# First weights ahead of the activations, their parts on two DMA queues, and the row norm spread inside the third tile

## The chip, the core and the metric

The kernel runs on one core of a Trainium2 chip. The metric is the device time of one execution in microseconds (us); of three runs the median counts. A core has five engines that run their own instruction streams and meet at semaphores: TensorE (PE, matrix products), VectorE (DVE), ScalarE (ACT), GpSimd (POOL) and SyncE (SP), which here only issues DMAs. "PEld" is the load of the stationary matrix of a product.

## The reference

Two small blocks of layers run one after the other on a sequence of 256 tokens (272 with 16 meta tokens in the first), with a model width of 1024, all in float32. What matters here is how the first block begins:

```python
h = jnp.concatenate([meta, x], axis=1)               # 272 x 1024
u = rmsnorm(h, mix_norm[layer])                      # x * rsqrt(mean(x^2) + eps) * gain
z = jnp.einsum('bld,de->ble', u, w_in[e])
hq, hf, hi, hg, cq, ckv, kr = jnp.split(z, IN_SPLITS, axis=-1)
o_a = hgrn2_mixer(hq, hf, hi, hg, lower_bounds[e], hgrn_out_norm[e])
o_b = mla_mixer(cq, ckv, kr, ...)
mix = jnp.einsum('ble,ed->bld', jnp.concatenate([o_a, o_b], axis=-1), w_out[e])
```

`hgrn2_mixer` turns `hf` into a decay (absolute values, exponentials, logarithms), sums it along the sequence in one scan, and works on chunks of 64 positions in levels of 1, 2, 4, 8, 16 and 32. Everything after this stage (the MLPs, a pooling layer, and the second block with a convolution and an attention) is some 1100 us of matrix products with the same helpers.

## The kernel before

**Layout.** The activations stand transposed: `X` is 128 x 8 x 272, the feature in the partition and in the middle index `j`, the token along the row. A product in float32 is made of three in a faster format: `UH` holds the high part of x times gain, `UL` the rest, and each weight unit is split into `WH` and `WL`. `products` (L367) issues for each of 8 blocks `k` the three matmuls UH,WH, UL,WH and UH,WL, so 24 matmuls of 272 columns to a 128-column tile of the result.

**Weights.** Weights come in units of up to 128 x 1024 floats (512 KB), one for each tile. Unit n goes by DMA from `wpack` into one of 4 buffers `RAW` (`load_unit`, L336), ACT copies it into one of 7 buffers `WH` (`act_split`, L345), and DVE writes `WL` = RAW - WH (`dve_split`, L352). The load of unit n waits until `WL` of unit n-4 is written. All of SP's DMAs are issued in the order of its program.

**The root.** The division by the root mean square comes after the product. ACT squares x in four pieces (`square`, L435), DVE adds them up (`add_squares`, L445), and PE sums over the partitions with matmuls against a column of ones (`root_begin` and `root_end`, through L449). ACT takes the square root (L480, L481), DVE the reciprocal (L487, L488), PE spreads it over all partitions (`root_spread`, L495), ACT copies it into `RR` (`root_keep`, L503). A tile's result is then multiplied by `RR` on its way out of PSUM (`divided`, L1061). Its 8 banks of PSUM are handed out in turn.

**The order at the start.** SP issues x whole, the gains, an identity matrix, then units 0 to 3 and a table of constants `C`. ACT waits for x, then works through squares, the eight `UH`, the root, `RR`, and only then splits units 0 to 3. DVE follows in the same order. PE makes the sums, the spread, and then the tiles: hf 0 to 3, hq 0 to 3, cq 0 and 1, ckv 0, the first attention level, ckv 1, and so on, with one level after every further tile. Behind the hf tiles a chain on ACT and DVE forms the decay (L936 to L951, L1257 to L1275), then the scan (L1278), then six rounds of exponents and operands for the levels (L1070 to L1109).

`keep_going(t, n)` (L398) issues n matmuls of ones by ones, 256 columns wide, whose result nobody reads. `preload` (L507) is a one-column activation that makes ACT load its table early. `act_split(a, n)` and `dve_split(v, n)` split all units below n that are not yet split.

Of the kernel before, what the change touches and what calls it, by code (L numbers as in the profile page):

```python
# [8 lines left out]
T = 272  # L9
# [3 lines left out]
NR = 4  # L13
# [92 lines left out]
NG = _at  # L106
# [171 lines left out]
def program(nc, xin, pin, gains, cst, wpack, out):  # L278
# [13 lines left out]
    with ctx:  # L292
# [28 lines left out]
        def g(name, j=0, p=128):  # L321
            return G[0:p, GAT[name] + j:GAT[name] + j + 1]
# [8 lines left out]
        def load_unit(s, n):  # L331
            w = width(units[n])
            src = wpack[offs[n]:offs[n] + 128 * w].rearrange("(p n) -> p n", p=128)
            if n >= NR:
                s.wait_ge("wl", n - NR)
            s.e.dma_start(RAW[n % NR][:, 0:w], src).then_inc(*s.mark_dma(f"raw{n % NR}", n))  # L336
# [135 lines left out]
        def root_sum(t, st, i, w, freed):  # L472
            root_begin(t, st, i, w, freed)
            root_end(t, st, i, w)
# [43 lines left out]
        def sync_start(s):  # L518
            s.e.dma_start(X[:, :, :], xin).then_inc(*s.mark_dma("x"))
            s.e.dma_start(G[:, :], gains).then_inc(*s.mark_dma("g"))  # L520
            s.e.dma_start(ID[:, :], cst[:, CAT["id"]:CAT["id"] + 128]).then_inc(*s.mark_dma("id"))
            for n in range(NR):
                load_unit(s, n)

# [77 lines left out]
        def tensor_mixer(t):  # L602
            u_ready = (lambda k: ("ul", "m", k))

            def project(key, js, freed):
                for j in js:
                    n = unit_at[key, j]
                    z = len(units[n][4])
                    b = banks.take(t, (key, j), (freed, key, j))
                    products(t, PS[0:z, b, 0:T], n, pairs, 0, z, xh_full, xl_full, u_ready).then_inc(*t.mark("mix", key, j))  # L610
                    sig.also(("used", n), ("mix", key, j))

            def values(uu, i):
# [166 lines left out]

            root_sum(t, "m", 0, T, ("rk", "m"))
            root_spread(t, "m", T)
            project("hf", range(4), "ev")
            project("hq", range(4), "ev")
# [94 lines left out]
        def scalar_mixer(a):  # L879
# [41 lines left out]

            a.wait_ge("g")
            a.wait_ge("ones", 2)
            a.wait_ge("x")
            for p in range(4):
                square(a, "m", 0, p, X[:, 2 * p:2 * p + 2, :], T)
            for j in range(8):
                split_hi(a, ("m", j), UH[:, j, :], X[:, j, :], g("mix0", j))
            root_sqrt(a, "m", T)
            root_keep(a, "m", 0, T)  # L930
            act_split(a, 4)
            a.wait_ge("lb", 0)
# [124 lines left out]
        def vector_mixer(v):  # L1057
# [169 lines left out]

            v.wait_ge("g")
            v.wait_ge("x")
            for p in range(4):  # L1230
                add_squares(v, "m", 0, p, T)
            for j in range(8):
                split_lo(v, ("m", j), UL[:, j, :], X[:, j, :], g("mix0", j), UH[:, j, :])
            root_recip(v, "m", T)
            lbg = G[:, GAT["lb"]:GAT["lb"] + 4]
            v.e.tensor_tensor(LO, lbg, lbg, ALU.subtract).then_inc(*v.mark("lb", 0))
            dve_split(v, 4)
            v.wait_ge("rr", "m")
# [1472 lines left out]
        def sync_program(s):  # L2711
            sync_start(s)
            s.e.dma_start(C[:, :], cst[:, 128:NCA]).then_inc(*s.mark_dma("c"))
            for n in range(NR, NU):
                load_unit(s, n)
            for p in range(4):
                s.wait_ge("x2", "end", p)
                s.e.dma_start(out[:, 2 * p:2 * p + 2, :], X[:, 2 * p:2 * p + 2, NM:T]).then_inc(*s.mark_dma("out", p))
            s.wait_ge("out", 3)
# [95 lines left out]
```

## Time and profile before

| | us |
|---|---|
| three runs | 1288.32, 1290.06, 1290.20 |
| median | 1290.06 |
| the profiled execution, its own time | 1293.58 |
| its span, first to last instruction | 1291.7 |
| PE busy | 1255.8 |
| DVE busy | 896.4 |
| ACT busy | 739.2 |

Busy time of an engine says how full it is over the whole program; which engine is waited for changes from stage to stage. Times in the rows further down are counted from the first instruction. In a timeline a row with xN is N instructions of one kind in a row, its second number is their time together, and consecutive instructions overlap a little, so the step from one start to the next is shorter than one instruction's duration. What stands in brackets is the idle time before the row and what ended it.

### The profile page before, as it was taken

To read this page: it belongs to the slowest core of one execution; us is meant where nothing else is said; L and a number is where in the kernel's file an instruction comes from. 1 tells how busy PE (TensorE), PEld (TensorE's weight loads), DVE (VectorE), ACT (ScalarE), POOL (GpSimd) and SP (SyncE) were. 2 spreads that over 40 slices of the span, in tenths; PEclk is the share of its full clock that TensorE was granted. 3 is DMA by queue.
4 is the path that set the end of the run, shared out by engine and by line. 5 is a ranking of instruction groups with operands and counts; after the bars stand their busy time and mean duration, and the time that the engine had idled before them with its cause. 6 is when DMAs were issued, how large, how long until landed. Compare 5 with 4: busy or idle time off the path is not lost.

```text
span 1291.7 us, 24686 instructions
## 1 busy us (share of the span) xinstructions
PE 1255.8 (97%) x10317; PEld 1232.7 (95%) x10317; DVE 896.4 (69%) x1549; ACT 739.2 (57%) x1262; POOL 6.4 (0%) x16
## 2 busy tenths in 40 slices
PE   5999999999999999999999999999999999999997
PEld 5989889999999999999999999999999899999997
DVE  4896456765456666444775799965788767999655
ACT  5854355654445666334545666664766766665644
POOL 1000000000000000000000000000000000000000
PEclk9999799999999999999999999999999999999999
DMA  6223124655553565554564566665364335655630
GB/s 246 94 82 115 65 82 147 213 169 190 166 164 114 193 184 184 190 181 154 180 197 131 171 196 194 190 205 163 101 207 164 103 115 169 197 192 186 217 118 34
DMA packets 58891, 205.54 MB, mean 159 GB/s; under 512 B 6515, under 2 KB 8860, under 8 KB 58524
## 3 DMA queue, kind: packets, MB, share of 16 engines
q1 hardware_dynamic: 57104, 201.77, 47.9%
q10 hardware_dynamic: 1676, 2.19, 0.6%
q8 instruction: 82, 1.34, 0.4%
q14 instruction: 29, 0.24, 0.1%
HBM read 202.87 MB, written 1.06 MB: 158 GB/s over the span
## 4 chain that ended last, share of the span: by engine, by line
PE 87%; ACT 5%; DVE 5%; DMA 1%; issue 1%; ACTq 0%; DVEq 0%
PE PS L367 70%; PE PS L415 6%; PE PS L378 2%; PE PS L449 2%; DVE WL L352 1%; ACT WH L345 1%; PE PS L398 1%; PE PS L2301 1%; PE PS L495 1%; ACT EE L2459 1%; ACT L507 1%; PE PS L637 1%; PE PS L2368 0%; PE PS L668 0%; DMA RAW<-wpack 0%
## 5 line engine op out<-in xcount | busy, mean ns | idle before, releaser
L352 DVE TENSOR_TENSOR WL<-RAW,WH 128x1024 fp32r<-128x1024 f32 (+2 forms) x385 | 460.4, 1201 | 218.8 <-ACT WH L345 218.4
L345 ACT ACTIVATE WH<-RAW 128x1024 fp32r<-128x1024 f32 (+2 forms) x385 | 392.4, 1038 | 230.6 <-PE PS L367 197.3
L367 PE MATMUL PS<-UH,WH 128*128 128x256 f32 (+2 forms) x1576 | 447.4, 284 | 3.5 <-DVE WL L352 2.7
L367 PE MATMUL PS<-UH,WL 128*128 128x256 f32 (+2 forms) x1576 | 447.2, 284 | 0.0
L367 PE MATMUL PS<-UL,WH 128*128 128x256 f32 (+2 forms) x1576 | 447.2, 284 | 0.0
L367 PEld LDWEIGHTS PS<-UH,WH 128*128 128x128 f32 (+1 forms) x1576 | 297.8, 189 | 4.3 <-DVE WL L352 3.0
L367 PEld LDWEIGHTS PS<-UH,WL 128*128 128x128 f32 (+1 forms) x1576 | 298.1, 189 | 0.0
L367 PEld LDWEIGHTS PS<-UL,WH 128*128 128x128 f32 (+1 forms) x1576 | 296.3, 188 | 0.0
L367 PE MATMUL PS<-HL,WH 128*128 128x272 f32 (+1 forms) x512 | 145.8, 285 | 0.0
L367 PE MATMUL PS<-HH,WH 128*128 128x272 f32 (+1 forms) x512 | 145.7, 285 | 0.0
L367 PE MATMUL PS<-HH,WL 128*128 128x272 f32 (+1 forms) x512 | 145.4, 284 | 0.0
L367 PE MATMUL PS<-FH,WH 128*128 128x256 f32 x352 | 98.6, 280 | 0.0
L367 PE MATMUL PS<-FL,WH 128*128 128x256 f32 x352 | 98.5, 280 | 0.0
L367 PE MATMUL PS<-FH,WL 128*128 128x256 f32 x352 | 98.4, 280 | 0.0
L367 PEld LDWEIGHTS PS<-HH,WL 128*128 128x128 f32 x512 | 96.6, 189 | 0.0
L367 PEld LDWEIGHTS PS<-HL,WH 128*128 128x128 f32 x512 | 96.3, 188 | 0.0
L367 PEld LDWEIGHTS PS<-HH,WH 128*128 128x128 f32 x512 | 96.1, 188 | 0.0
L415 PE MATMUL PS<-UH,WH 128*128 128x256 f32 (+1 forms) x256 | 74.1, 290 | 1.2 <-DVE UL L515 1.0
L415 PE MATMUL PS<-UH,WL 128*128 128x256 f32 (+1 forms) x256 | 72.0, 281 | 0.0
L415 PE MATMUL PS<-UL,WH 128*128 128x256 f32 (+1 forms) x256 | 72.0, 281 | 0.0
L367 PEld LDWEIGHTS PS<-FH,WH 128*128 128x128 f32 x352 | 66.2, 188 | 0.0
L367 PEld LDWEIGHTS PS<-FL,WH 128*128 128x128 f32 x352 | 66.2, 188 | 0.0
(392 smaller groups left out, 1931.8 us busy)
## 6 DMA issues: line engine op xcount, KB each, us to landing
RAW<-wpack SPq DMA_DIRECT2D x363, 512.0 KB, 3.8
RAW<-wpack SPq DMA_DIRECT2D x16, 384.0 KB, 3.5
RAW<-wpack SPq DMA_DIRECT2D x6, 256.0 KB, 2.6
X<-xin SPq DMA_DIRECT2D x1, 1088.0 KB, 5.0
C<-cst SPq DMA_DIRECT2D x1, 1072.0 KB, 10.0
HB<-bias_rows ACTq DMA_DIRECT2D x1, 1024.0 KB, 6.2
out<-X SPq DMA_DIRECT2D x4, 256.0 KB, 2.3
VF<-cst ACTq DMA_DIRECT2D x1, 512.0 KB, 3.8
```

The costliest lines, as they stand in the source:

```text
L345: a.e.activation(WH[n % NH][:, 0:w], RAW[n % NR][:, 0:w], ACT.Copy).then_inc(*a.mark("wh", n))
L352: v.e.tensor_tensor(WL[n % NH][:, 0:w], RAW[n % NR][:, 0:w], WH[n % NH][:, 0:w].bitcast(f32), ALU.subtract).then_inc(*v.mark("wl", n))
L367: ins = t.e.matmul(o, part(n, hw, kw, a, b), x(kx), start=first and not i and not p, stop=last and i == len(kcs) - 1 and p == 2)
L378: ins = t.e.matmul(o, x(kx), part(n, hw, kw, 0, w), start=not i and not p, stop=i == len(kcs) - 1 and p == 2)
L398: t.e.matmul(PS[:, b, 0:256], ONER[:, :], ONER[:, :].unsqueeze(1).to_broadcast([128, 2, 128]), start=True, stop=True)
L415: ins = t.e.matmul(PS[:, b, 0:w], part(n, hw, k, 0, 128), x_(k), start=k == 0 and p == 0, stop=k == 7 and p == 2)
L449: return t.e.matmul(o, src[:, m, a:z], ONE[:, 0:1], start=first and m == 0, stop=last and m == 1)
L495: ins = t.e.matmul(PS[:, b, a:z], rooted(st, x).to_broadcast([128, 128]), ID[:, 0:z - a], start=True, stop=True)
L507: a.e.activation(SM[:, 60:61], EPS[:, 0:1], func)
L637: ins = t.e.matmul(PS[:, b + x // 4, 128 * (x % 4):128 * (x % 4) + 128], kb[:, hh, a:z], qb[:, hh, a:z], start=True, stop=True)
L2301: ins = t.e.matmul(PS[:, b, 0:256], x[:, k, 128 * i:128 * i + 128], part(n, hw, kw, 0, 256), start=k == 0 and p == 0, stop=k == 7 and p == 2)
L2459: ins = a.e.activation(e, e, ACT.Exp, bias=s[:, 2 * i + m:2 * i + m + 1], scale=-1.0, accum_out=s[:, 4 + 2 * i + m:5 + 2 * i + m])
```

## The change

The change touches only the beginning.

- SP issues unit 0, then the second quarter of x, unit 1, the fourth quarter, the identity matrix, unit 2, the rest of the gains, unit 3. The table `C` moves behind unit 5.
- ACT issues three DMAs of its own: the eight columns of the gains that the first norm needs, and the first and third quarter of x. It then loads the table of the square root, splits unit 0, and makes the eight `UH`, with unit 1 split after the sixth. Squares come after that, then units 2 and 3, then the root.
- DVE takes the same order: unit 0, the eight `UL`, unit 1, the sums of squares, units 2 and 3, the reciprocal.
- PE begins with 24 matmuls of ones, makes tile hf 0 with one matmul of ones between two blocks and six behind it, then hf 1, the sums of the root (with 4 matmuls of ones in their midst), hf 2 with the spread in its middle, hf 3, and goes on as before.

```diff
         def sync_start(s):
-            s.e.dma_start(X[:, :, :], xin).then_inc(*s.mark_dma("x"))
-            s.e.dma_start(G[:, :], gains).then_inc(*s.mark_dma("g"))
+            load_unit(s, 0)
+            s.e.dma_start(X[:, 2:4, :], xin[:, 2:4, :]).then_inc(*s.mark_dma("xp1"))
+            load_unit(s, 1)
+            s.e.dma_start(X[:, 6:8, :], xin[:, 6:8, :]).then_inc(*s.mark_dma("xp3"))
             s.e.dma_start(ID[:, :], cst[:, CAT["id"]:CAT["id"] + 128]).then_inc(*s.mark_dma("id"))
-            for n in range(NR):
-                load_unit(s, n)
+            load_unit(s, 2)
+            s.e.dma_start(G[:, 8:NG], gains[:, 8:NG]).then_inc(*s.mark_dma("g"))
+            load_unit(s, 3)
...
+            def first_tile():
+                b = banks.take(t, ("hf", 0), ("ev", "hf", 0))
+                for k in range(8):
+                    ins = products(t, PS[:, b, 0:T], unit_at["hf", 0], [(k, k)], 0, 128, xh_full, xl_full, u_ready, k == 0,
+                                   k == 7)
+                    if k < 7:
+                        keep_going(t, 1, done=("ones",))
...
+                keep_going(t, 6, done=("ones",))
+            def tile_with_root():
...
+                products(t, PS[:, b, 0:T], n, pairs[0:4], 0, 128, xh_full, xl_full, u_ready, True, False)
+                root_spread(t, "m", T)
+                products(t, PS[:, b, 0:T], n, pairs[4:8], 0, 128, xh_full, xl_full, u_ready, False, True).then_inc(
...
-            root_sum(t, "m", 0, T, ("rk", "m"))
-            root_spread(t, "m", T)
-            project("hf", range(4), "ev")
+            t.wait_ge("ones", 0)
+            keep_going(t, 24)
+            first_tile()
+            project("hf", (1,), "ev")
+            root_begin(t, "m", 0, T, ("rk", "m"))
+            keep_going(t, 4, done=("ones",))
+            root_end(t, "m", 0, T)
+            tile_with_root()
+            project("hf", (3,), "ev")
...
-            a.wait_ge("g")
-            a.wait_ge("ones", 2)
-            a.wait_ge("x")
+            a.e.dma_start(G[:, 0:8], gains[:, 0:8]).then_inc(*a.mark_dma("gm"))
+            for p in (0, 2):
+                a.e.dma_start(X[:, 2 * p:2 * p + 2, :], xin[:, 2 * p:2 * p + 2, :]).then_inc(*a.mark_dma(f"xp{p}"))
+            preload(a, ACT.Sqrt)
+            act_split(a, 1)
+            a.wait_ge("gm")
+            for j in range(8):
+                a.wait_ge(f"xp{j // 2}")
+                split_hi(a, ("m", j), UH[:, j, :], X[:, j, :], g("mix0", j))
+                if j == 5:
+                    act_split(a, 2)
             for p in range(4):
                 square(a, "m", 0, p, X[:, 2 * p:2 * p + 2, :], T)
-            for j in range(8):
-                split_hi(a, ("m", j), UH[:, j, :], X[:, j, :], g("mix0", j))
+            act_split(a, 4)
+            a.wait_ge("ones", 2)
             root_sqrt(a, "m", T)
             root_keep(a, "m", 0, T)
-            act_split(a, 4)
+            a.wait_ge("g")
...
+            dve_split(v, 1)
+            v.wait_ge("gm")
+            for j in range(8):
+                v.wait_ge(f"xp{j // 2}")
+                split_lo(v, ("m", j), UL[:, j, :], X[:, j, :], g("mix0", j), UH[:, j, :])
+            dve_split(v, 2)
             for p in range(4):
                 add_squares(v, "m", 0, p, T)
-            for j in range(8):
-                split_lo(v, ("m", j), UL[:, j, :], X[:, j, :], g("mix0", j), UH[:, j, :])
+            dve_split(v, 4)
             root_recip(v, "m", T)
+            v.wait_ge("g")
...
             for n in range(NR, NU):
                 load_unit(s, n)
+                if n == NR + 1:
+                    s.e.dma_start(C[:, :], cst[:, 128:NCA]).then_inc(*s.mark_dma("c"))
```

The instructions of ACT, from its first on, in the program before. `WH<-RAW` is the split of a weight unit, `UH<-X,G` the high part of x times gain, `ACC` and `SQ` are the squares, `RS` the root; in brackets is what the row waits for:

```order
L435 ACT_TABLE_LOAD [waits s_x,s_ones]
L435 ACTIVATE ACC<-X 128x544 [waits s_g]
L435 ACTIVATE SQ<-X 128x544 x2
L435 ACTIVATE SQ<-X 128x544 [waits s_acc]
L511 ACTIVATE UH<-X,G 128x272 x8
L480 ACT_TABLE_LOAD
L480 ACTIVATE RS<-PS,EPS 16x1 [waits s_sum]
L481 ACTIVATE RS<-PS,EPS 128x2
L503 ACTIVATE RR<-PS 128x272 [waits s_rsp]
L345 ACTIVATE WH<-RAW 128x1024 [waits s_raw0]
```

And ACT in the changed program, from its first split on (its three DMA issues and the load of the table stand before it):

```order
L345 ACTIVATE WH<-RAW 128x1024 [waits s_raw0]
L511 ACTIVATE UH<-X,G 128x272 [waits s_xp0,s_gm]
...
L511 ACTIVATE UH<-X,G 128x272
L345 ACTIVATE WH<-RAW 128x1024 [waits s_raw1]
L511 ACTIVATE UH<-X,G 128x272 [waits s_xp3]
L511 ACTIVATE UH<-X,G 128x272
L435 ACTIVATE ACC<-X 128x544
L435 ACTIVATE SQ<-X 128x544 x2
L435 ACTIVATE SQ<-X 128x544 [waits s_acc]
L345 ACTIVATE WH<-RAW 128x1024 [waits s_raw2]
L345 ACTIVATE WH<-RAW 128x1024 [waits s_raw3]
L480 ACTIVATE RS<-PS,EPS 16x1 [waits s_sum,s_ones]
```

Units 0 to 3 moved ahead of the root, the squares behind the `UH`, and one of the two table loads is gone.

PE from its first matmul on, in the program before (`ONE,ACC` and `ONE,SQ` are the sums of the root, `ID,RS` is its spread, `UH,WH` the first matmul of tile hf 0):

```order
L449 MATMUL PS<-ONE,ACC 128x1 [waits s_acc]
L449 MATMUL PS<-ONE,ACC 128x1 x3
L449 MATMUL PS<-ONE,SQ 128x1 [waits s_sq]
L449 MATMUL PS<-ONE,SQ 128x1 x3
L449 MATMUL PS<-ONE,ACC 16x1 x2
L449 MATMUL PS<-ONE,SQ 16x1 x2
L495 MATMUL PS<-ID,RS 128x16 [waits s_id,s_rr]
L495 MATMUL PS<-ID,RS 128x128 x2
L367 MATMUL PS<-UH,WH 128x272 [waits s_ul,s_wl]
```

PE in the changed program at the same sums, which now stand between tiles hf 1 and hf 2 (`ONE` are the matmuls of ones, the last row the first matmul of hf 2):

```order
L449 MATMUL PS<-ONE,ACC 128x1 [waits s_acc]
L449 MATMUL PS<-ONE,ACC 128x1 x3
L398 MATMUL PS<-ONE 128x256 x4
L449 MATMUL PS<-ONE,SQ 128x1 [waits s_sq]
L449 MATMUL PS<-ONE,SQ 128x1 x3
L449 MATMUL PS<-ONE,ACC 16x1 x2
L449 MATMUL PS<-ONE,SQ 16x1 x2
L367 MATMUL PS<-UH,WH 128x272 [waits s_wl]
```

Before, these sums and the spread stood ahead of the first tile; now two tiles, or 48 matmuls, run before them.

## Rows read from the trace of the kernel before

**Rows 1.** The page, part 1: busy time by engine.

```profile
PE 1255.8 (97%) x10317; PEld 1232.7 (95%) x10317; DVE 896.4 (69%) x1549; ACT 739.2 (57%) x1262; POOL 6.4 (0%) x16
```

**Rows 2.** Waits of PE, 0 to 170 us: us in total, times, longest.

```profile
PE PS L449 <- DVE ACC L445: 10.1, 1, 10.1
PE PS L367 <- DVE WL L352: 2.7, 1, 2.7
```

**Rows 3.** The chain that ended last, from the start: start us, us, what.

```profile
0.74 5.03 DMA X<-xin
...
13.22 1.28 ACT L480
...
19.55 34.80 PE PS L367 x264
...
73.91 0.72 DVE KB L1085
...
93.14 2.84 PE PS L668 x24
```

**Rows 4.** Windows at the start: PE busy, PEclk, DMA share, GB/s.

```profile
3.00:4.00 1.00, 0.00 (x0) 1.00 1.00 418
...
20.00:21.00 1.00, 1.00 (x6) 1.00 0.40 90
```

**Rows 5.** The page, part 6: DMA issues, KB each, us to landing.

```profile
RAW<-wpack SPq DMA_DIRECT2D x363, 512.0 KB, 3.8
```

**Rows 6.** Timeline, 9 to 23 us: start us, us, engine line op.

```profile
9.81 3.39 ACT L511 ACTIVATE UH<-X,G 128x272 fp32r<-128x272 f32 x8
...
15.21 1.65 PE L495 MATMUL PS<-ID,RS 128*128 128x16 f32 x6 [1.24 <-DVE RS L488]
...
17.19 3.88 ACT L345 ACTIVATE WH<-RAW 128x1024 fp32r<-128x1024 f32 x4
18.27 4.63 DVE L352 TENSOR_TENSOR WL<-RAW,WH 128x1024 fp32r<-128x1024 f32 x4 [3.05 <-ACT WH L345]
...
19.95 0.43 PE L367 MATMUL PS<-UL,WH 128*128 128x272 f32 x1
...
20.17 0.43 PE L367 MATMUL PS<-UH,WL 128*128 128x272 f32 x1
...
22.54 0.29 PE L367 MATMUL PS<-UL,WH 128*128 128x272 f32 x1
...
22.66 0.29 PE L367 MATMUL PS<-UH,WL 128*128 128x272 f32 x1
```

**Rows 7.** Timeline of DVE, 33 to 50 us.

```profile
33.20 0.44 DVE L1061 TENSOR_TENSOR LF<-PS,RR 128x272 f32<-128x272 f32 x1 [1.45 <-PE PS L367]
...
39.25 0.44 DVE L1061 TENSOR_TENSOR Q<-PS,RR 128x272 f32<-128x272 f32 x1 [2.58 <-PE PS L367]
...
48.33 1.29 DVE L1275 TENSOR_TENSOR LF<-LF,B 128x1088 f32<-128x1088 f32 x1 [0.20 <-ACT B L951]
```

**Rows 8.** Timeline of ACT, 33 to 45 us.

```profile
33.68 1.11 ACT L936 ACTIVATE B<-LF 128x1088 f32<-128x1088 f32 x1 [1.07 <-DVE LF L1061]
...
44.11 1.11 ACT L948 ACTIVATE B<-B 128x1088 f32<-128x1088 f32 x1 [0.17 <-DVE B L1266]
```

**Rows 9.** Waits of DVE, 39 to 94 us: us in total, times, longest.

```profile
DVE KB L1085 <- PE PS L643: 0.9, 2, 0.6
```

**Rows 10.** Timeline of PE, near the program's end.

```profile
1278.26 1.36 PE L398 MATMUL PS<-ONE 128*128 128x256 f32 x10
...
1279.46 0.95 PE L449 MATMUL PS<-ONE,ACC 128*128 128x1 f32 x8
```

**Rows 11.** Windows of 2 us: PE busy, PEclk, DMA share, GB/s.

```profile
136.00:138.00 2.00, 2.00 (x17) 1.00 0.65 205
...
140.00:142.00 2.00, 2.00 (x10) 0.50 0.56 221
...
152.00:154.00 2.00, 2.00 (x9) 0.98 0.00 0
```

More of the change, by code:

```diff
@@ L611, in project @@
                     sig.also(("used", n), ("mix", key, j))
+            def first_tile():
[5 more added lines that the diff above has]
+                        keep_going(t, 1, done=("ones",))
+                ins.then_inc(*t.mark("mix", "hf", 0))
+                sig.also(("used", unit_at["hf", 0]), ("mix", "hf", 0))
+                keep_going(t, 6, done=("ones",))
+            def tile_with_root():
+                n = unit_at["hf", 2]
+                b = banks.take(t, ("hf", 2), ("ev", "hf", 2))
+                products(t, PS[:, b, 0:T], n, pairs[0:4], 0, 128, xh_full, xl_full, u_ready, True, False)
+                root_spread(t, "m", T)
+                products(t, PS[:, b, 0:T], n, pairs[4:8], 0, 128, xh_full, xl_full, u_ready, False, True).then_inc(
+                    *t.mark("mix", "hf", 2))
+                sig.also(("used", n), ("mix", "hf", 2))
             def values(uu, i):
@@ L1226, in normed @@
                     *v.mark("rope", "k"))
-            v.wait_ge("g")
-            v.wait_ge("x")
+            dve_split(v, 1)
[4 more added lines that the diff above has]
+            dve_split(v, 2)
             for p in range(4):
                 add_squares(v, "m", 0, p, T)
-            for j in range(8):
-                split_lo(v, ("m", j), UL[:, j, :], X[:, j, :], g("mix0", j), UH[:, j, :])
+            dve_split(v, 4)
             root_recip(v, "m", T)
+            v.wait_ge("g")
             lbg = G[:, GAT["lb"]:GAT["lb"] + 4]
             v.e.tensor_tensor(LO, lbg, lbg, ALU.subtract).then_inc(*v.mark("lb", 0))
-            dve_split(v, 4)
             v.wait_ge("rr", "m")
@@ L2712, in sync_program @@
             sync_start(s)
-            s.e.dma_start(C[:, :], cst[:, 128:NCA]).then_inc(*s.mark_dma("c"))
             for n in range(NR, NU):
                 load_unit(s, n)
+                if n == NR + 1:
+                    s.e.dma_start(C[:, :], cst[:, 128:NCA]).then_inc(*s.mark_dma("c"))
             for p in range(4):
```

## The prediction

> **What bounds the kernel now.** I read the page first: PE is busy for 1255.8 of 1291.7 us [rows 1], so time is to be won only where PE stands idle or runs slowly. The waits of PE show where it is idle early on: 10.1 us until the squares are summed and 2.7 us until the first weights are split [rows 2]. The chain that ended last gives the order in which the start is bound: x lands at 5.77 us, ACT and DVE work for 14 us, a table load of 1.28 us among it, and the first product of a tile begins at 19.55 [rows 3]. Units 0 to 3, the weights of the first four tiles, have long been in memory by then; their splits only stand last in ACT's and DVE's programs, from 17.19 and 18.27 us on [rows 6].
>
> From 19.55 to 73.8 us the chain is PE's alone. From 73.91 to 93.14 us it is DVE's: the operands of the levels, and PE waits for them [rows 3]. The waits of DVE show how long that engine has been full: between 39 and 94 us it waits 2.6 us before the row at 39.25, 0.2 us before the row at 48.33 and 0.9 us elsewhere [rows 7, 9], 3.7 us in 55. So what PE gains at the start counts only as far as this DVE work moves forward too. What sets its beginning is ACT's chain on the four hf tiles, which starts at 33.68 us, right behind the last hf tile leaving PSUM at 33.20 [rows 7, 8]. That chain decides the gain, more than PE's first product.
>
> **The change part by part.**
>
> *First data.* The first DMA brings its data 5.03 us after its issue, 1.09 MB [rows 3]; from 3 us on 418 GB/s flow [rows 4], and 3.8 us is the median from issue to landing of a unit [rows 5]. Unit 0 (0.52 MB) is now first on SP. With the same start and the same lag behind the last byte as x it would land near 4.5 us alone; if it shares the 418 GB/s evenly with ACT's two quarters of x (0.28 MB each) it lands near 5.4; behind both it lands at 5.8. I take 5.4 us, the middle way, with 4.5 and 5.8 as the ends. No row shows a DMA of rows as thin as the eight gain columns (32 bytes each); it has until 6.4 us and costs nothing up to there.
>
> No row has two queues at once. The Trainium skill, DMA: Bandwidth & Descriptors, section "Issuing engines are not separate DMA queues", says that DMAs issued by several engines run on the same 16 DMA engines and interleave, so that only issue time is saved. By that rule unit 0 shares; queues that add up would put it at 4.5 us and the end 0.9 us earlier. No row here shows which.
>
> *ACT.* Steps from start to start are 0.97 us for a split (3.88 / 4), 0.41 for one `UH` (3.39 less one overlap, over 8; DVE's `UL` keep the same step behind them) [rows 6]. Unit 0's split ends at 6.4, six `UH` follow to 8.9, unit 1 to 9.8, the last two `UH` end at 10.7, squares follow. Three quarters of x land by about 6.5 and the fourth by 8.3, each ahead of its use.
>
> *DVE.* Its split steps 1.14 us (4.63 / 4 less the overlap) [rows 6]. `WL` of unit 0 is ready at 7.6, the first `UL` at 8.1, the last at 11.2, `WL` of unit 1 at 12.4, the sums of squares at 13.8, units 2 and 3 at 15.9 and 17.0.
>
> *PE.* A quick matmul of a tile steps 0.125 us, a slow one 0.22 (22.54 to 22.66, and 19.95 to 20.17) [rows 6], so a tile takes 3.0 or 5.4 us. A quick matmul of ones costs 0.12 (1.36 less one overlap, over 10), four sums over the full width, eight rows in the trace, 0.95 [rows 10]. The first product starts at 8.1. Its blocks come every 0.41 with `UL`, or every 0.5 with the matmul of ones between them, so hf 0 ends at 11.6, when the last `UL` is there. Six ones bring it to 12.4, hf 1 runs to 15.4, the sums with four ones take 2 x 0.95 + 0.5 + 0.2 = 2.6, to 18.0. The first half of hf 2 (1.5) hides the root and the reciprocal, before which PE stood idle for 1.24 us [rows 6]. The spread cost 1.65 slow [rows 6] and is put at 0.8 quick; hf 2 ends at 21.8 and hf 3 at 24.8. Before, the last hf tile left PE at 33.2: PE is 8.3 us ahead. The added 41 matmuls of ones cost about 0.7 + 0.5 + 0.8 us of this; the first 24 lie in idle time.
>
> *The decay chain.* After the spread ACT copies `RR` (to 20.7), loads the exponential's table (1.28 [rows 3]) and does one small activation, to 22.2. Only then it splits unit 4. DVE now has four splits and four hf tiles in turn from 23.2 us: 4 x 1.14 + 3 x 0.36 + 0.44 = 6.1 us, so hf 3 leaves PSUM at 29.3, not at 25.3 as PE would allow. Before it was 33.64. The chain starts 4.4 us earlier than its 33.68 [rows 8]. It does the same work as before, but no longer waits at 39.25 for hq 1 [rows 7], which is out of PE by 31; that gives 0.2 to 0.4 us more for the part from 44.11 on [rows 8]. So the DVE work from 48.33 on [rows 7] moves by 4.7 us. PE, 8.3 us ahead, now waits for operands and units 8 to 13 between 43 and 65 us, some 3 us in all, where it had no waits, and gives its lead back. At most 0.9 us of DVE's own waits [rows 9] goes, because PE is earlier; I count 0.1. The sum at 93 us is **4.8 us**, and PE is the bound behind it, with the same instructions.
>
> *Loads.* SP's queue now holds `C` (1.1 MB, 2.6 us at 418 GB/s) between units 5 and 6. Behind it wait unit 6, issued at 15.9, and unit 7, at 17.0; they land by 21, and their splits come at 24 and 25, so it costs nothing. `C` itself is first used behind eleven tiles. `WL` of unit 4, at 24.3, frees the buffer of unit 8, which lands 3.8 us later [rows 5], at 28.1; ACT splits it ahead of the decay chain, to 29.1, just before 29.3. This is the tightest spot: each microsecond more costs 0.8. ACT's three issues lie ahead of any work. One table load less (1.28 us at 13.22 [rows 3]) sits in the idle start now. The Trainium skill, ScalarE: Activation LUTs, section "What ACT_TABLE_LOAD costs", adds 1.38 us of drain to each switch. The row does not show it; by the page the load that is left on the path, for the exponential, would cost that much more and the gain were 3.4 us.
>
> **The sum.** The profiled execution took 1293.58 us, 1.9 more than its span; less 4.8 it is 1288.8. The three runs without a profile have a median of 1290.06, which is 3.5 lower, so **1285.3 us**.
>
> **The rivals.**
>
> *PE runs the first tiles slowly (B).* The matmuls of ones end near 5.7 us and PE then idles until 8.1. In the rows the tile that follows an idle PE begins with a step of 0.22 us and reaches 0.125 only after 2.7 us [rows 6], and the sums and the spread before it did not help. For it: the idle time is as long as the 2.7 us in [rows 2]. Against it: 24 matmuls of full width come before. If the pace is slow until 11.5, four blocks take 0.9 instead of 0.5 and the tile ends at 13.7, everything behind it 2.0 us later: gain 2.8, 1287.3 us. The granted clock can't tell it beforehand: it reads 1.00 in the window from 20 to 21 us, where the step is the slow one [rows 4].
>
> *All of PE's lead counts (C).* If DVE's order leaves less behind than I think, and the decay chain starts by PE's hf 3, the gain is 8.3 us, 1281.8. For it: PE bounds the chain up to 73.8. Against: DVE's 3.7 us of waits in 55. An early return from the slow clock would give as much.
>
> *Slower: the slow clock spreads (E).* In the stretch after the last hg tile, with small matmuls, the granted clock falls to 0.50, which is 1.2 GHz, and PE is back at 2.4 GHz at 152 us; at 136 to 138 us it was still 1.00 [rows 11]. All this moves by 5 us. If the clock falls at the stretch's first matmul and comes back only at its last (136 to 156 in the times of before), 2.6 and 4 us of work take twice as long: 6.6 us lost, 1.8 slower, 1291.9. It decides the sign when more than 4.8 of these 6.6 us are hit. For it: nothing in the code ties the fall to one instruction. Against: three runs within 1.9 us, so it hardly wanders.
>
> *The change does nothing (D).* If unit 0 or the thin gains land at 9 us instead of 5.4, or PE's new waits in 43 to 65 us slow it, the gain is 1 us: 1289.
>
> **How the numbers follow.** The forecast has 0.47, B 0.22, C 0.12, D 0.09, E 0.10. A difference under 0.2% (2.6 us) can hardly be told from none. Faster takes all of the forecast and of C and 0.4 of B: 0.68. Same takes the rest of B, and D: 0.21. Slower is E: 0.11. The forecast's own range is 1284.2 to 1286.8 (unit 0 from 4.5 to 5.8, the drain). Down to C and up through B and D to 1289.5 about 0.2 is left outside, so the range is 1281.8 to 1289.5.
>
> **What would show it.** Right: PE's first product near 8 us; the last hf tile out of PSUM near 29, and ACT's L936 at 29.3; DVE's L1275 near 43.6; short waits of PE between 43 and 65; PE's L668 at 88.3. Wrong: the step of the matmuls in the first tile at 0.22 us (B); hf 3 leaving right behind PE (C); unit 0 landing past 6; a stretch at clock 0.50 longer or shorter than 138.6 to 152.

## The result and the profile after

The changed kernel has a median of 1287.49 us over 12 runs (1283.12 to 1290.37), the kernel before, run on the same chip beside it, 1292.93 us over 12 (1287.20 to 1300.19). The ratio is 0.9958, with a 95% interval of 0.9940 to 0.9976: 5.4 us faster, between 3.1 and 7.8. The profiled execution took 1288.19 us at a span of 1286.4, against 1293.58 at 1291.7 before.

PE's busy time on the page, for [rows 1]:

```profile
PE 1260.6 (98%) x10358; PEld 1236.8 (96%) x10358; DVE 896.4 (70%) x1549; ACT 737.9 (57%) x1262; POOL 6.4 (0%) x16
```

PE is busy for 4.8 us more in a span that is 5.3 us shorter, and has 41 instructions more, the ones. Its waits from 0 to 170 us, in total, times, longest, for [rows 2]:

```profile
PE PS L367 <- DVE UL L515: 2.4, 1, 2.4
PE PS L367 <- DVE CL L1154: 1.5, 1, 1.5
PE PS L367 <- DVE WL L352: 1.3, 1, 1.3
```

The 10.1 us before the sums of squares are gone. PE waits 2.4 us for the first `UL`, and the waits for `CL` and for a `WL`, both between 43 and 66 us, are new. The chain that ended last, from the start, for [rows 3]:

```profile
0.74 4.30 DMA RAW<-wpack
...
43.32 1.77 ACT B L991 x4
...
46.44 2.44 DVE B L1321
...
89.69 2.84 PE PS L694 x24
92.52 4.46 PE PS L378 x24
...
98.30 2.83 PE PS L378 x24
...
104.05 4.00 PE PS L378 x24
```

PE no longer carries the chain alone up to 73 us: ACT carries it from 30.95 to 45.12 us (its last row is shown), DVE behind that. PE's sums over the heads (L694, before L668) start at 89.69 instead of 93.14 us, 3.45 earlier. Right behind them the same 24 products take 4.46 us once, 4.00 once and 2.83 in between. ACT's timeline (start us, us), for [rows 6, 8]:

```profile
5.07 1.06 ACT L345 ACTIVATE WH<-RAW 128x1024 fp32r<-128x1024 f32 x1 [1.42 <-DMA RAW<-wpack]
6.51 1.76 ACT L511 ACTIVATE UH<-X,G 128x272 fp32r<-128x272 f32 x4 [0.39 <-DMA X<-xin]
8.49 0.93 ACT L511 ACTIVATE UH<-X,G 128x272 fp32r<-128x272 f32 x2 [0.22 <-DMA X<-xin]
...
19.68 0.25 ACT L480 ACTIVATE RS<-PS,EPS 16x1 f32<-16x1 f32 x1 [3.52 <-PE PS L449]
...
21.99 0.40 ACT L503 ACTIVATE RR<-PS 128x272 f32<-128x272 f32 x1 [1.92 <-PE PS L495]
22.41 1.28 ACT L973 ACT_TABLE_LOAD   x1
23.70 0.21 ACT L973 ACTIVATE SMALL<-SMALL 128x4 f32<-128x4 f32 x1
23.81 3.89 ACT L345 ACTIVATE WH<-RAW 128x1024 fp32r<-128x1024 f32 x4
29.50 1.06 ACT L345 ACTIVATE WH<-RAW 128x1024 fp32r<-128x1024 f32 x1 [1.80 <-DMA RAW<-wpack]
30.95 1.12 ACT L976 ACTIVATE B<-LF 128x1088 f32<-128x1088 f32 x1 [0.38 <-DVE LF L1101]
```

Two quarters of x arrive a little behind the time at which ACT wants them (0.39 and 0.22 us). ACT then waits 3.52 us for PE's sums and 1.92 for its spread, splits units 4 to 7 without a wait, and the decay chain (L976, before L936) starts at 30.95 us, 2.73 earlier than at [rows 8]. PE's timeline at the first tile, for the last four rows of [rows 6]:

```profile
0.99 4.54 PE L398 MATMUL PS<-ONE 128*128 128x256 f32 x24 [0.99 <-POOL EPS L531]
7.94 0.56 PE L367 MATMUL PS<-UH,WH 128*128 128x272 f32 x1 [2.41 <-DVE UL L515]
8.30 0.43 PE L367 MATMUL PS<-UL,WH 128*128 128x272 f32 x1
8.53 0.43 PE L367 MATMUL PS<-UH,WL 128*128 128x272 f32 x1
```

The ones end at 5.53 us, PE idles for 2.41, and the first tile runs with a step of 0.23 us (8.30 to 8.53), the slow one. The windows (us, PE busy, PEld, DVE, ACT, POOL, PEclk, DMA share, GB/s), for [rows 11]:

```profile
8.00:10.00 2.00, 2.00 (x9) 2.00 (x10) 1.92 (x5) 1.78 (x4) 0.00 (x0) 0.50 1.05 408
10.00:12.00 2.00, 2.00 (x14) 2.00 (x13) 1.14 (x4) 2.00 (x5) 0.00 (x0) 0.74 1.04 423
...
94.00:96.00 2.00, 2.00 (x11) 2.00 (x11) 2.00 (x3) 1.22 (x2) 0.00 (x0) 0.50 0.68 223
...
140.00:142.00 2.00, 2.00 (x17) 1.85 (x16) 0.00 (x0) 0.00 (x0) 0.00 (x0) 1.00 0.50 193
...
152.00:154.00 2.00, 1.89 (x24) 1.15 (x23) 1.51 (x13) 2.00 (x9) 0.00 (x0) 1.00 0.00 0
...
156.00:158.00 2.00, 2.00 (x6) 1.52 (x5) 1.93 (x9) 2.00 (x10) 0.00 (x0) 0.55 0.00 0
```

The stretch at 1.2 GHz that stood at 138.6 to 152 us before is not there. There are others instead: in the first tile, twice between 92 and 108 us, at 154 to 158 us, and near 922 to 929 us. The difference of the two profiles, followed along the same instructions:

| | before | after | gained so far |
|---|---|---|---|
| PE, head sums (L668, L694) | 93.14 | 89.69 | 3.45 |
| PE, output stage begins (L827, L859) | 135.91 | 135.54 | 0.37 |
| PE, KN,QN (L741, L767) | 148.45 | 143.50 | 4.95 |
| PE, SQ,ONE (L713, L739) | 159.77 | 153.02 | 6.75 |
| span | 1291.7 | 1286.4 | 5.3 |

So 3.45 us come from the start of the kernel. The 3.1 us lost behind it and the 4.6 us won in the output stage go with the clock: the output stage took 12.54 us before, most of it at 0.50, and takes 7.96 now. Another 1.8 us are won up to 159.77, where the first KN,QN products of before still ran at 0.50, and 1.4 us are lost again on balance behind that: 1.7 us between 918 and 945 us, around a slow stretch of the changed kernel's profile, with 0.6 won back by 957. So the 5.3 us between the two spans are 3.45 us of the start and 1.9 us that follow the slow stretches of either profile.

### The profile page after: what moved, and what is told of

The parts are those of the page before. It is cut to its first block, busy times and chain, and to the rows that moved or that the text cites. A ratio compares the mean times of both kernels' runs of the same rounds, so it can differ in the third digit from the quotient of the medians.

```text
span 1286.4 us, 24776 instructions
## 1 busy us (share of the span) xinstructions
PE 1260.6 (98%) x10358; PEld 1236.8 (96%) x10358; DVE 896.4 (70%) x1549; ACT 737.9 (57%) x1262; POOL 6.4 (0%) x16
## 4 chain that ended last, share of the span: by engine, by line
PE 88%; DVE 6%; ACT 5%; issue 1%; DMA 0%; ACTq 0%; DVEq 0%
PE PS L367 68%; PE PS L415 7%; PE PS L378 2%; PE PS L449 2%; ACT WH L345 1%; DVE WL L352 1%; PE PS L398 1%; PE PS L2344 1%; PE PS L495 1%; ACT EE L2502 1%; ACT L507 0%; PE PS L694 0%; PE PS L2411 0%; DVE ATT L1144 0%; DVE EE L2600 0%
```

## The experiments

My theory behind the prediction was that the start of the decay chain on ACT sets the gain. Its rivals were that PE's lead counts (C), or that the pace of the first tiles decides (B). The edits are against the changed kernel, that of e3 against the kernel before. All marks are us from the start of the profiled execution: the copy of `RR` (ACT L503), the start of the decay chain (ACT L976), the head sums (PE L694). The lines are those of the changed kernel; in the others the same instruction can stand some lines off. The last two columns belong to that same execution. A run of before stood beside e1 to e4 (1290.37 us) and one beside e5 to e9 (1298.85); as it spreads that much, single times decide nothing, and I read the marks.

| | first product | RR | L976 | L694 | L976 to L694 | clock | time |
|---|---|---|---|---|---|---|---|
| before | 19.55 | 16.90 | 33.68 | 93.14 | 59.46 | 0.992 | 1293.58 |
| changed | 7.94 | 21.99 | 30.95 | 89.69 | 58.74 | 0.989 | 1288.19 |
| e1_no_ones | 7.31 | 20.54 | 29.50 | 88.25 | 58.75 | 0.998 | 1282.18 |
| e2_44_ones | 9.40 | 22.40 | 31.36 | 90.11 | 58.75 | 0.990 | 1287.53 |
| e3_dma_only | 19.98 | 17.33 | 35.73 | 94.66 | 58.93 | 0.986 | 1299.65 |
| e4_order_only | 11.08 | 25.64 | 34.59 | 93.35 | 58.76 | 0.989 | 1290.86 |
| e5_early_splits | 7.30 | 20.60 | 26.59 | 85.37 | 58.78 | 0.996 | 1281.00 |
| e6_one_queue | 7.73 | 24.16 | 33.11 | 91.85 | 58.74 | 0.991 | 1289.26 |
| e7_spread_first | 7.20 | 21.02 | 29.98 | 89.08 | 59.10 | 0.994 | 1282.66 |
| e9_pe_late | 7.30 | 20.71 | 29.67 | 88.45 | 58.78 | 0.997 | 1282.66 |
| e10_changed_again | 7.34 | 20.90 | 29.86 | 88.57 | 58.71 | 0.993 | 1284.47 |
| e11_no_ones_timed | 7.36 | 21.10 | 30.06 | 88.77 | 58.71 | 0.988 | 1287.63 |
| e12_early_splits_timed | 7.22 | 21.39 | 27.38 | 86.11 | 58.73 | 0.990 | 1283.73 |
| e13_early_no_ones | 7.32 | 20.54 | 26.53 | 85.24 | 58.71 | 0.996 | 1280.43 |

**e1_no_ones.** All matmuls of ones at the start are left out.

```diff
-                    if k < 7:
-                        keep_going(t, 1, done=("ones",))
...
-                keep_going(t, 6, done=("ones",))
...
-            keep_going(t, 24)
+            keep_going(t, 0)
...
-            keep_going(t, 4, done=("ones",))
```

> The changed kernel without any of its 41 matmuls of ones at the start (24 ahead, 7 between blocks, 6 behind the first tile, 4 in the sums). Marks of the changed kernel: first product at 7.94 us, first product of tile hf 1 at 13.96, ACT L976 at 30.95, DVE L1318 at 45.12, the sums L694 at 89.69 (with about 2 us of slow clock around it). Theory 1 (the ones bring nothing, since PE idles 2.4 us after the first 24 and goes slow anyway): first product at 7.9 again in the slow pace, hf 1 starts 1 to 1.5 us earlier because 13 ones are gone, L976 at 29.2 to 29.7. Rival (the ones keep PE quick): the slow pace lasts longer than 11 us, hf 1 starts at 14.5 or later, L976 later than 30.95.

PE's timeline of this kernel:

```profile
7.31 0.56 PE L367 MATMUL PS<-UH,WH 128*128 128x272 f32 x1 [7.31 <-DVE UL L515]
7.67 0.43 PE L367 MATMUL PS<-UL,WH 128*128 128x272 f32 x1
7.90 0.43 PE L367 MATMUL PS<-UH,WL 128*128 128x272 f32 x1
```

The first tile is slow, as in the changed kernel's first profile, and still `RR` comes 1.45 us earlier there. 0.63 of it is the earlier first product, since unit 0 landed at 4.44 instead of 5.07 us; the other 0.8 us are no more than the ones behind hf 0 and in the sums cost themselves (10 at 0.12). Without them the first tile ends near 12.4 us and PE waits 0.49 us for `WL` of unit 1, which is there at 12.88, so the pace of the tile costs nothing here. L976 came where it was expected (29.50 us).

**e2_44_ones.** The warm-up is made long enough to reach the first product.

```diff
-            keep_going(t, 24)
+            keep_going(t, 44)
```

> 44 instead of 24 matmuls of ones ahead of the first tile, so that PE has no idle time before it (24 ended at 5.53 us, 20 more at 0.12 end near 7.9). Theory 1 (the idle time of 2.4 us is what made the clock fall at 7.8): granted clock 1.00 from 7 to 12 us, the first tile in the quick pace and bound by the last UL at 11.8; hf 1 starts at 12.9 instead of 13.96, L976 at 29.9, L1318 at 44.1. Rival (the clock falls whatever PE did before): slow pace up to 11 us as in the changed kernel, all marks as there.

The first tile ran with the quick step from its first block, but the start was lost to something else, in ACT's timeline:

```profile
8.08 2.59 ACT L511 ACTIVATE UH<-X,G 128x272 fp32r<-128x272 f32 x6 [2.51 <-DMA X<-xin]
```

The first quarter of x was there at 8.08 us only, 1.6 us later than in the changed kernel with the same DMAs. From the first `UH` to `RR` it took 14.32 us (22.40 - 8.08), against 15.48 in the changed kernel and 14.61 in e1. So a quick first tile is worth about 1.2 us against the slow one with ones, and 0.3 against none at all. The expected marks (hf 1 at 12.9, L976 at 29.9) were missed, 14.36 and 31.36, by that late quarter.

**e3_dma_only.** Only SP's and ACT's DMAs are those of the changed kernel; ACT, DVE and PE work in the order of before.

```diff
-            s.e.dma_start(X[:, :, :], xin).then_inc(*s.mark_dma("x"))
-            s.e.dma_start(G[:, :], gains).then_inc(*s.mark_dma("g"))
+            load_unit(s, 0)
+            s.e.dma_start(X[:, 2:4, :], xin[:, 2:4, :]).then_inc(*s.mark_dma("xp1"))
+            load_unit(s, 1)
...
             for p in range(4):
+                a.wait_ge(f"xp{p}")
                 square(a, "m", 0, p, X[:, 2 * p:2 * p + 2, :], T)
```

> The kernel before with the new DMAs alone (two queues, x in four parts, C later); ACT, DVE and PE keep the old order, squares and root first. Theory 1 (the gain is the order of the splits, and x is late by the weights ahead of it): the last quarter of x lands near 9 us instead of 5.8, the first product of a tile near 21.5 instead of 19.55, L1318's counterpart near 50 instead of 48.33, the sums over the heads near 95 instead of 93.14. Rival (two queues and parts of x bring the gain): first product before 19.5, the marks earlier than before.

The decay chain starts 2.05 us later than before. ACT's timeline shows why:

```profile
30.25 1.06 ACT L345 ACTIVATE WH<-RAW 128x1024 fp32r<-128x1024 f32 x1 [3.75 <-DMA RAW<-wpack]
33.02 1.06 ACT L345 ACTIVATE WH<-RAW 128x1024 fp32r<-128x1024 f32 x1 [1.72 <-DMA RAW<-wpack]
```

Units 4 to 7 are loaded late, because their buffers come free late, and `C` (1.1 MB) now stands in the queue between units 5 and 6: ACT waits 3.75 and 1.72 us for the next two. In the changed kernel, with `C` in the same place, ACT splits units 4 to 7 without a wait, since their buffers come free earlier. The new place of `C` is part of this edit and was not tested by itself; but the first product (19.98 against 19.55; 21.5 was expected) and `RR` (17.33 against 16.90) are 0.43 us later than before ahead of it, so the new DMAs gain nothing there either.

**e4_order_only.** The orders of ACT, DVE and PE are the new ones, the DMAs those of before, with x whole and first.

```diff
-            load_unit(s, 0)
-            s.e.dma_start(X[:, 2:4, :], xin[:, 2:4, :]).then_inc(*s.mark_dma("xp1"))
...
+            s.e.dma_start(X[:, :, :], xin).then_inc(*s.mark_dma("x"))
+            s.e.dma_start(G[:, :], gains).then_inc(*s.mark_dma("g"))
...
+            for n in range(NR):
+                load_unit(s, n)
```

> The changed kernel's order on ACT, DVE and PE with the DMAs of before (x whole, the gains, the identity, units 0 to 3, C, all on SP). Theory 1: unit 0 is behind 1.4 MB and lands near 7.5 us instead of 5.07, so the first product comes near 10.3, L976 at 33 (30.95 in the changed kernel, 33.68 before), L694 at 92 (89.69; 93.14 before): the order without the DMAs keeps about a third of the gain. Rival (the order is all): L976 within 0.7 us of 30.95.

```profile
8.20 1.06 ACT L345 ACTIVATE WH<-RAW 128x1024 fp32r<-128x1024 f32 x1 [5.96 <-DMA RAW<-wpack]
```

ACT stands until 8.20 us for unit 0, which lies behind x, and the decay chain starts at 34.59 us, 0.9 later than before. The expectation, a third of the gain, was missed: neither half of the change gains anything alone (e3: +2.05, e4: +0.91); together they start the chain 2.7 to 3.8 us earlier. Each is one execution, and e4's first tile ran slowly. With e10's 22.52 us from the first product to L976 in place of its 23.51, e4 would start the chain at 33.6 us, the time of before; that is an estimate.

**e5_early_splits.** ACT and DVE split units 4 and 5 ahead of the root, while they wait for PE's sums.

```diff
-            act_split(a, 4)
+            act_split(a, 6)
...
-            dve_split(v, 4)
+            dve_split(v, 6)
```

> The changed kernel, with units 4 and 5 split by ACT and DVE ahead of the root, in the time in which ACT waits for the sums (3.5 us idle before L480 at 19.68) and DVE for the root. Theory 1 (the chain RR, table load, split of unit 4, four splits and four evacuations sets the start of the decay chain): the first evacuation comes right behind RR, at 22.4 instead of 26.0, only two splits (2.3 us) stand between the four, so L976 comes when PE has hf 3, near 28.5 to 29 instead of 30.95, and L694 near 87.3 instead of 89.69. Rival (PE's lead or something else sets it): L976 stays within 0.5 us of 30.95.

The chain starts at 26.59 us, 6.0 behind `RR` instead of 9.0, and the head sums follow with the same 58.8 us. The order of ACT and DVE decides; PE's first product did not move (7.30 against 7.34 in e10). Against e10, whose first tile is quick too, L976 is 3.3 us earlier.

**e6_one_queue.** ACT's three DMAs go to SP's queue.

```diff
+            s.e.dma_start(G[:, 0:8], gains[:, 0:8]).then_inc(*s.mark_dma("gm"))
             load_unit(s, 0)
-            s.e.dma_start(X[:, 2:4, :], xin[:, 2:4, :]).then_inc(*s.mark_dma("xp1"))
+            for p in (0, 1):
+                s.e.dma_start(X[:, 2 * p:2 * p + 2, :], xin[:, 2 * p:2 * p + 2, :]).then_inc(*s.mark_dma(f"xp{p}"))
             load_unit(s, 1)
...
```

> The changed kernel with all DMAs on SP: eight gain columns, unit 0, first and second quarter of x, unit 1, third and fourth, and the rest as it was. Theory 1 (both queues share the same bandwidth; the second one only saves issue time, and splits the order): unit 0 lands near 4.6 us (5.04 with two queues), the first quarter near 5.4 to 6 (6.4), the first product at 7.3 to 8 (7.94), all marks within 0.8 us. Rival (two queues carry more): first product 1 us or more later, L976 past 32.

```profile
4.86 1.06 ACT L345 ACTIVATE WH<-RAW 128x1024 fp32r<-128x1024 f32 x1 [2.62 <-DMA RAW<-wpack]
5.82 1.80 ACT L511 ACTIVATE UH<-X,G 128x272 fp32r<-128x272 f32 x4
9.95 0.93 ACT L511 ACTIVATE UH<-X,G 128x272 fp32r<-128x272 f32 x2 [2.33 <-DMA X<-xin]
```

Unit 0 and the first half of x are as early as with two queues; the third quarter, behind unit 1, is awaited for 2.33 us. A second queue brings no faster start of the data, it brings another order. The first product (7.73) is within what theory 1 allowed, L976 (33.11) is not; it lies where the rival had it, but not for the rival's reason. `RR` is 2.2 us later than in the changed kernel's first profile: 1.5 us is this wait (9.95 against 8.49), and 1.5 more is the wait for the spread (3.46 us against 1.92), which falls in a slow stretch; the quick first tile gives 0.8 back. This kernel's windows:

```profile
20.00:22.00 2.00, 2.00 (x18) 1.98 (x16) 0.48 (x5) 0.40 (x2) 0.00 (x0) 0.66 1.00 377
22.00:24.00 2.00, 2.00 (x11) 2.00 (x11) 0.00 (x0) 0.00 (x0) 0.00 (x0) 0.50 0.31 125
```

**e7_spread_first.** The spread of the root stands ahead of hf 2 instead of in its middle.

```diff
+                root_spread(t, "m", T)
                 products(t, PS[:, b, 0:T], n, pairs[0:4], 0, 128, xh_full, xl_full, u_ready, True, False)
-                root_spread(t, "m", T)
```

> The changed kernel with the spread of the root ahead of tile hf 2, not in its middle: PE waits for root and reciprocal. Theory 1: PE idles about 0.8 us (the 1.24 us of before less the table load, which is gone), RR comes 1.0 us earlier (it no longer waits for 12 matmuls, 1.7 us), so L976 comes 0.7 to 1.0 us earlier, at 30 to 30.3, although PE is later by 0.8, since ACT's and DVE's chain sets the start and not PE. Rival (PE's tiles set the pace): L976 0.8 us later, at 31.7.

The spread in this kernel, and then in e10, the changed kernel as it is:

```profile
19.34 1.65 PE L495 MATMUL PS<-ID,RS 128*128 128x16 f32 x6 [0.79 <-DVE RS L488]
```

```profile
20.04 0.83 PE L495 MATMUL PS<-ID,RS 128*128 128x16 f32 x6
```

PE waits 0.8 us for the reciprocal, as expected, and the spread starts 0.70 us earlier. `RR` is no earlier all the same (21.02 against 20.90), because a slow stretch from about 18.7 to 25.5 us doubled the spread from 0.83 to 1.65 us. So this execution does not decide between the two places of the spread: at the quick pace `RR` would have come some 0.7 us earlier (an estimate from these rows), with PE later by the wait.

It shows something else. PE lost its lead in that stretch, and DVE waits for it as in [rows 7]:

```profile
35.18 0.44 DVE L1101 TENSOR_TENSOR Q<-PS,RR 128x272 f32<-128x272 f32 x1 [2.58 <-PE PS L367]
```

With that wait L976 to L694 is 59.10 us and not 58.7.

**e9_pe_late.** PE is held back by 20 matmuls of ones (2.4 us) behind hf 3.

```diff
             project("hf", (3,), "ev")
+            keep_going(t, 20, done=("ones",))
```

> The changed kernel with 20 matmuls of ones (2.4 us of PE) between tiles hf 3 and hq 0. Theory 1 (DVE's work sets the end of the stage, and PE has a lead that it gives back in waits of 2.8 us for CL L1154 and WL L352): L976 at 30.95 as before, L1318 at 45.1, L694 at 89.7 to 90.4; the waits on CL and WL shrink to under 1 us. Rival (PE's lead counts in full): L694 at 92.1, 2.4 us later.

PE's waits of this kernel:

```profile
PE PS L367 <- DVE UL L515: 2.1, 2, 1.6
...
PE PS L367 <- DVE CL L1155: 1.0, 1, 1.0
```

The extra 2.4 us vanish: the wait for `WL` is gone and that for `CL` is shorter, 1.8 of them. L694 is at 88.45 us, against 88.57 in e10, and L976 to L694 is 58.78 us. That ends rival C: of PE's lead behind the hf tiles the last 2.4 us are worth nothing. A PE that is later still does count, as e7 shows.

**e10_changed_again.** The changed kernel, unedited, in twelve runs beside the next three.

> The changed kernel itself, timed beside the next three. Theory: the distance from L976 to L694 is 58.75 us again (fixed by DVE's work), L694 between 88.3 and 89.7 as unit 0 and x land and as the first tile runs in the quick or the slow pace; span and granted clock go together: mean clock 0.996 to 0.998 gives 1281 to 1283, 0.989 to 0.991 gives 1286 to 1289. Rival (the distance depends on PE): other than 58.6 to 58.9.

1286.98 us, ratio 0.9962 (0.9938 to 0.9986) to 34 runs of before with a median of 1292.96: the result again. Its profiled execution differs from the first one. PE's ones, ACT's split of unit 0 and PE's first products, from the timeline of this run:

```profile
0.99 5.49 PE L398 MATMUL PS<-ONE 128*128 128x256 f32 x24 [0.99 <-POOL EPS L531]
...
4.47 1.06 ACT L345 ACTIVATE WH<-RAW 128x1024 fp32r<-128x1024 f32 x1 [0.83 <-DMA RAW<-wpack]
...
7.34 0.36 PE L367 MATMUL PS<-UH,WH 128*128 128x272 f32 x1 [0.86 <-DVE UL L515]
7.54 0.29 PE L367 MATMUL PS<-UL,WH 128*128 128x272 f32 x1
7.67 0.29 PE L367 MATMUL PS<-UH,WL 128*128 128x272 f32 x1
```

Unit 0 landed 0.6 us earlier, the ones ended 0.95 us later, the idle time between them shrank to 0.86 us, and the tile ran with the quick step (0.13). The gain at L694 is 4.57 us here, 3.45 in the first profile.

**e11_no_ones_timed.** The kernel of e1, in twelve runs.

> The changed kernel without its 41 matmuls of ones at the start, timed. Theory (the first tile waits for UL and the second for WL of unit 1 anyway, so pace and ones ahead decide nothing, while the 10 ones behind them cost up to 1.2 us): equal to the changed kernel or up to 1.5 us faster, ratio to it 0.9985 to 1.000. Rival (the ones earn their place): 1 to 3 us slower than the changed kernel.

1288.16 us, ratio 0.9973 (0.9949 to 0.9998), 1.2 us above e10 where up to 1.5 us less was expected, with intervals 6 us wide. Neither a gain nor a cost of the ones can be told.

**e12_early_splits_timed.** The kernel of e5, in eleven runs.

> The changed kernel with units 4 and 5 split ahead of the root, timed. Theory: L976 is 3 us earlier than in the changed kernel (26.59 against 29.5 to 30.95) and all of it reaches the end: 3 us (0.25%) faster than the changed kernel. Rival (the gain is taken back later): within 0.1% of it.

1283.33 us, ratio 0.9928 (0.9902 to 0.9954): 3.65 us below e10 (3 were expected), and the lowest median of all. Its interval and e10's still overlap a little. ACT's timeline:

```profile
13.63 3.88 ACT L345 ACTIVATE WH<-RAW 128x1024 fp32r<-128x1024 f32 x4
19.08 0.25 ACT L480 ACTIVATE RS<-PS,EPS 16x1 f32<-16x1 f32 x1 [1.57 <-PE PS L449]
...
27.38 1.12 ACT L976 ACTIVATE B<-LF 128x1088 f32<-128x1088 f32 x1 [1.23 <-DVE LF L1101]
```

Four splits instead of two stand before the root, and the wait for the sums is 1.57 instead of 3.52 us. L976 starts 2.5 us earlier than in e10 and L694 follows with 2.46, although the first tile of this execution was slow and e10's quick.

**e13_early_no_ones.** Both edits together, in twelve runs.

> Both: units 4 and 5 split ahead of the root, and none of the 41 matmuls of ones at the start. Theory: L976 near 26, since the root now is bound by PE's sums, which come 0.5 to 1.2 us earlier without ones; L694 near 84.7; 3.5 to 4 us faster than the changed kernel, the fastest of the four. Rival (DVE and ACT, now fuller, delay the root by their splits): L976 at 27 or later, no faster than with the ones.

1284.61 us, ratio 0.9948 (0.9921 to 0.9974). It had the earliest L694 of all (85.24; 84.7 was expected), but not the lowest median, and is not told apart from e12.

## Why the prediction came out as it did

The forecast was 1285.3 us, 4.8 less than its base; measured were 1287.49, inside the range, and 5.4 less than the runs beside it. Step by step:

**The bound.** Right. The prediction said that the decay chain's start decides the gain, not PE's first product. From L976 to L694 twelve executions take 58.71 to 58.93 us, with L976 anywhere from 26.53 to 35.73. Before took 59.46 and e7 59.10, and both have DVE waiting 2.58 us for hq 1 [rows 7]. I had put 0.2 to 0.4 us on that wait; 0.7 us are gone. It is not more because ACT takes over. Right behind that place DVE waits for it in the changed kernel (us in total, times, longest):

```profile
DVE K L1300 <- ACT B L982: 2.3, 1, 2.3
```

So up to 45.12 us ACT's chain sets the distance, as the prediction had it, and DVE's work behind that.

**First data.** Forecast 5.4 us (4.5 to 5.8) for unit 0. It landed by 5.07 in the first profile and at 4.33 to 4.51 in the nine others with two queues in which ACT waits for it. Queues that share evenly were the wrong middle (and by its own numbers that was 5.65 and not 5.4 us: 1.04 MB at 418 GB/s, where 1.09 land at 5.77): unit 0 went nearly as if alone, and x came after it, the first quarter at 5.9 to 6.5 us and once at 8.08. The step "each ahead of its use" failed for two quarters, by 0.2 to 0.7 us each, and by 2.5 us once. The Trainium skill, DMA: Bandwidth & Descriptors, section "Issuing engines are not separate DMA queues", says that a second issuing engine adds no bandwidth. e6 agrees: one queue had unit 0 at 4.86 us, between these, and the windows from 8 to 12 us of the changed kernel show 408 and 423 GB/s from two queues, against 418 from one [rows 4].

**The first tile.** Forecast 8.1 us for the first product, measured 7.94 (7.34 in e10). What came next in the first profile is rival B word for word: idle from 5.5, a step of 0.23, quick from 11.1 us on, hf 1 at 13.96 instead of 12.4. In e10, the same kernel, it is the forecast. The sizes of both were good: B's gain was put at 2.8, 2.4 of it at L976, and measured 2.73 at L976 and 3.45 at L694; the forecast's was 4.8, and e10 shows 4.57 at L694. That one kernel does both was not foreseen. Over the profiles, the idle time behind the ones was 2.41 us where the first tile began slow, 1.74 in e12, where it turned slow within the first three products, and 0.86 to 1.62 us in e2, e5, e6, e7, e9 and e10, all quick. e4, at 5.15 us, was slow too, and so were e1, e11 and e13, which have no ones. Whether the idle time is the cause is not shown: only e2 set out to change it, and there it shrank to 1.11 us with a quick tile behind it.

**The chain to the decay.** Forecast: `RR` copied by 20.7, first `WL` at 23.2, 6.1 us to L976. Measured in the first profile: 22.4, 24.89, 6.06. The size was right to 0.1 us, so the 1.65 us at L976 (30.95 against 29.3) were lost ahead of it. About 1.1 of them are the slow first tile, since e10 with a quick one is at 29.86. The other 0.56 it keeps, although its first product is 0.76 us earlier than forecast: its last `UL` ends at 11.54 us instead of 11.2 and hf 1 begins at 12.9 instead of 12.4, behind the x that came late. The Trainium skill, ScalarE: Activation LUTs, section "What ACT_TABLE_LOAD costs", would add 1.38 us of drain to the load at 22.41. The trace disagrees: `RR` ends at 22.39, the load starts at 22.41 and lasts 1.28 us, and the next activation starts at 23.70.

**PE's waits.** Forecast some 3 us between 43 and 65, measured 2.8 (1.5 + 1.3). e9 shows that most of them are PE's lead given back.

**C.** Excluded by e9, and by e5, where ACT's and DVE's order alone moved L694 by 3.2 us against e10.

**D's cause, E.** Nothing that was waited for landed at 9 us. The slow stretch did not spread: 136 to 154 us is quick in the first profile. But slow stretches appear at 92 to 108, among the 128x256 products, at 154 to 158 and at 922 to 929 us. So E's premise, that the stretch belongs to these small matmuls alone, failed.

**The sum.** The step that was mis-sized is the last one: 3.5 us less than the profile's sum, from three runs at 1290.06. The twelve runs of before beside the changed kernel, of which these three are the first, gave 1292.93, and 34 more in the last comparison 1292.96. The three had a low base by chance, and their spread of 1.9 us told nothing of the 13 us (1286.93 to 1299.93) that 34 runs show. With the true base the forecast would have been 1288.1. That the sum on the profiled execution, 1288.8, came within 0.6 us of the changed kernel's 1288.19 is in part luck: 3.45 us were gained at the start and not 4.8, and the clock gave 1.9.

What spreads the runs is the mean clock that each was granted. Mean time of the runs at one clock, with their number; before, e10 and e12 ran side by side, the first twelve of the changed kernel in an earlier comparison:

| granted clock | before (34 runs) | changed (first 12) | e10 | e12 |
|---|---|---|---|---|
| 0.996 | 1287.64 (9) | 1283.87 (3) | 1281.96 (1) | |
| 0.993 | 1292.26 (1) | | 1284.47 (1) | 1281.12 (3) |
| 0.990 | 1293.93 (9) | 1288.43 (4) | 1287.55 (4) | 1283.97 (3) |
| 0.987 | 1297.64 (3) | | 1292.92 (1) | |

At one clock the change is worth 3.8 us (0.996) and 5.5 us (0.990) by the first twelve, and 5.7 us (0.996, one run) and 6.4 us (0.990) by e10. The 4.8 of the sum lies among them; closer it can't be told. The mean clock over the runs is 0.9916 for before (34 runs), 0.9913 for the changed kernel and 0.9915 for e10. So no change of the clock on average is seen, but twelve runs fix that mean only to about 0.001, which goes with about 1 us.

The slow stretches are not spread over the program at random. In nine of the twelve profiles with the new order one starts 1.8 to 3.9 us behind the start of L694; in six of these nine another follows 13.5 to 15.5 us behind it, and in seven one starts 833 to 835 us behind it. The one in the output stage stands in both profiles with the old order and in none of the twelve with the new: in e3 it lies at 144.7 to 158.4 us, begins in the same group of matmuls as before (the second round of `ATT,VT`), and is as long. One of e3's windows:

```profile
146.00:148.00 2.00, 2.00 (x10) 1.77 (x9) 0.00 (x0) 0.00 (x0) 0.00 (x0) 0.50 0.56 215
```

Not every run of before has it: 13.7 us at 0.50 in a span of 1291.7 bring the mean to 0.995 at most (an estimate), and 11 of the 34 were granted 0.996 or more. So whether the 6.4 us won from 135 to 160 us in the first pair of profiles are a draw or in part an effect of the new order is open, and so is the cause of the stretches; no experiment here moved one on purpose.

## What to carry to other kernels

Find the instruction from which the distance to the next bound is constant, and count only what moves it; here it was ACT's first step on the hf tiles. Two weight splits moved into ACT's idle time ahead of the root brought 2.46 us at L694, more than half of what the whole change brought there (4.57 in e10). The order of the engines and the order of the transfers belong together: neither half of this change paid alone. A base from three runs can be off by more than half the effect (2.9 of 5.4 us here), so compare profile with profile, and read the granted clock of each run beside its time.

## What the runs showed of the hardware

- One kernel's executions were granted mean clocks from 0.984 to 0.998, and 0.006 of it (0.996 against 0.990) went with 4.6 to 6.3 us of time. In a profile it appears as a few stretches at 0.50 (1.2 GHz) of about 3 to 14 us each, also where PE is busy without a gap (16.00 of the 16 us from 92 to 108, granted clock 0.79). They differ between executions of one kernel, but come back at the same few places of the program, on different chips. A stretch does not always cost its share: that at 154 to 158 us of the changed kernel's profile falls in a part that ACT and DVE set, and PE's products at 162 us are as far ahead of before as those at 153 (6.7 us).
- The windows from 1 to 7 us show a granted clock of 1.00 although 24 ones took 5.49 us in e10, against 1.36 us for ten near the end of the program [rows 10]: at the start the row does not tell the pace. Two of e10's windows:

```profile
2.00:3.00 1.00, 1.00 (x7) 1.00 (x6) 0.00 (x0) 0.86 (x1) 1.00 (x2) 1.00 0.81 226
...
5.00:6.00 1.00, 1.00 (x6) 1.00 (x6) 0.44 (x1) 0.55 (x2) 0.13 (x1) 1.00 1.01 408
```

- The first 512 KB landed between 4.33 and 5.07 us with the same DMAs, and a quarter of x between 5.9 and 8.1. The eight thin gain columns (4 KB in rows of 32 bytes) took 3.7 to 4.5 us from issue to landing on ACT's queue while the weights came on SP's, nearly as long as 512 KB (4.30), and 1.7 us at the head of the only queue in e6.
